# The sums of the second product's weight quarters, made by GpSimd beside the mixers instead of by VectorE before the product

## What is computed

```python
h = rms_norm(x, norm_w[layer]); proj = jnp.einsum('bsd,de->bse', h, w_in[layer])
(gq, gk, gv, glr, hq, hf, hi, xq, gate) = jnp.split(proj, split_idx, axis=-1)
# 4 heads of gated linear attention, with a gate from glr by a low-rank product,
# 4 recurrent heads (hgrn), 4 heads of cross attention on a memory of 256 tokens
mixed = jnp.concatenate([gla_o, hgrn_o, xo], axis=-1) * jax.nn.silu(gate)
x = x + jnp.einsum('bse,ed->bsd', mixed, w_out[layer])
```

```python
def sq_relu_mlp(h, w1, w2):
    return jnp.square(jax.nn.relu(h @ w1)) @ w2      # w1 1024 x 4096, w2 4096 x 1024
```

## Time and the profile before

| | us |
|---|---|
| median of 3 runs | 1999.69 |
| lowest and highest run | 1998.44, 2000.65 |
| the profiled execution, its own time | 1998.49 |
| its span, first to last instruction | 1996.7 |
| TensorE busy | 1964.0 (98%) |
| VectorE, ScalarE, GpSimd busy | 1254.3, 852.9, 927.4 |

### The profile page before, as it was taken

The page is one execution under the profiler, slowest core; times in us unless marked ns, Lnnn a source line. Parts: engine busy times, 40 slices in busy tenths (PEclk is TensorE's granted clock), DMA queues, the critical chain, the costliest instruction groups (busy, mean ns, idle before and its releaser), DMA issues.

```text
span 1996.7 us, 26700 instructions
## 1 busy us (share of the span) xinstructions
PE 1964.0 (98%) x10042; PEld 1649.4 (83%) x10042; DVE 1254.3 (63%) x2095; ACT 852.9 (43%) x1431; POOL 927.4 (46%) x584
## 2 busy tenths in 40 slices
PE   9999999999999999999999999999999999999997
PEld 7988988988988888888888777777788888888886
DVE  6264455446546365555579988896561845778856
ACT  5524232343543632121455557575643534333321
POOL 4521211112121334344428886686443855877851
PEclk9999999999999999999999999999999999999999
DMA  4301101011011596766335443334457886453432
GB/s 182 106 31 53 43 33 53 33 54 38 27 64 39 178 331 228 255 238 240 127 134 193 180 139 111 119 128 142 143 169 282 307 295 206 137 185 135 142 114 85
DMA packets 94047, 284.34 MB, mean 142 GB/s; under 512 B 10576, under 2 KB 10960, under 8 KB 93792
## 3 DMA queue, kind: packets, MB, share of 16 engines
q1 hardware_dynamic: 70736, 240.17, 35.0%
q10 hardware_dynamic: 23184, 42.48, 5.9%
HBM read 223.36 MB, written 59.24 MB: 142 GB/s over the span
## 4 chain that ended last, share of the span: by engine, by line
PE 59%; DVE 3%; ACT 3%; issue 2%; POOL 1%; DMA 0%; POOLq 0%; DVEq 0%; SPq 0%; ACTq 0%
PE B L1775 33%; PE B L2005 13%; PE B L1954 10%; PE B L2080 1%; DVE HB L2546 1%; POOL WL L3118 1%; PE B L2016 0%; ACT HB L2205 0%; DVE B L2546 0%; POOL CO L3177 0%; DMA SUMW<-wall 0%; DVE RES L2546 0%; DVE TM L2546 0%; ACT CO L2490 0%; PE B L1939 0%
## 5 line engine op out<-in xcount | busy, mean ns | idle before, releaser
L1775 PE MATMUL B<-HB,WH 128*128 128x512 f32 x2976 | 949.5, 401 | 6.3 <-ACT HB L2205 3.6
L1775 PEld LDWEIGHTS B<-HB,WH 128*128 128x128 f32 x2976 | 548.0, 189 | 129.2 <-issue 18.7
L1775 PE MATMUL B<-HB,WL 128*128 128x512 f32 x1488 | 578.0, 391 | 1.8 <-POOL WL L3118 1.8
L3118 POOL TENSOR_TENSOR WL<-RAW,WH 128x1024 fp32r<-128x1024 f32 x132 | 320.2, 2430 | 351.0 <-ACT WH L2205 349.3
L2205 ACT ACTIVATE WH<-RAW 128x1024 fp32r<-128x1024 f32 (+1 forms) x201 | 204.7, 1024 | 316.1 <-DMA RAW<-wall 298.4
L1775 PEld LDWEIGHTS B<-HB,WL 128*128 128x128 f32 x1488 | 279.6, 188 | 62.8 <-POOL WL L3118 3.1
L3116 POOL TENSOR_TENSOR WL<-RAW,WH 128x512 fp32r<-128x512 f32 x82 | 113.8, 1412 | 315.7 <-ACT WH L2205 315.6
L2546 DVE SCALAR_TENSOR_TENSOR B<-UP,vec,B 128x512 f32<-128x512 f32 x308 | 206.3, 747 | 0.0
L2546 DVE SCALAR_TENSOR_TENSOR RES<-B,modv,RES 128x512 f32<-128x512 f32 x204 | 148.0, 743 | 81.8 <-PE B L2005 59.1
L1838 PE MATMUL B<-WH,HB 128*128 128x256 f32 x768 | 153.2, 297 | 0.0
L3103 POOL TENSOR_TENSOR small<-small 128x4 f32<-128x4 f32 (+2 forms) x36 | 38.4, 1069 | 210.3 <-DVE small L2549 210.0
(11 more groups left out here) (270 smaller groups left out, 3330.5 us busy)
## 6 DMA issues: line engine op xcount, KB each, us to landing
RAW<-wall SPq DMA_DIRECT2D x172, 512.0 KB, 3.7
MODRAW<-wmod ACTq DMA_DIRECT2D x96, 256.0 KB, 4.9
WH<-parts SPq DMA_DIRECT2D x32, 512.0 KB, 3.2
WL<-parts SPq DMA_DIRECT2D x32, 512.0 KB, 4.1
hscr<-HR ACTq DMA_DIRECT2D x64, 256.0 KB, 3.2
HQ<-hscr SPq DMA_DIRECT2D x32, 512.0 KB, 6.4
SUMW<-wall SPq DMA_DIRECT2D x28, 512.0 KB, 7.3
sums<-SUMR SPq DMA_DIRECT2D x25, 512.0 KB, 5.9
```

Of the source, the lines that this page charges most:

```text
L1775: i = pe.matmul(bank, a[:, ks], hb(part, k, h), start=k == 0 and n == 0, stop=k == 7 and n == 2)
L3118: i = po.tensor_tensor(lo, raw, hi.bitcast(F32), ALU.subtract)
```

## The change

The sums move. The whole chain of load, four sums and store for each of the 28 units now runs beside the mixers, one unit at a time, in the tile GLR, from the place behind `gate_up` of head 3. Load, sums and store are placed 1.8, 1.6 and 1.6 planner us after one another. GpSimd makes the sums in place: S1 over A22, S3 over A21, S2 over A11, S4 over A12, so each unit keeps its four sums in the places of its quarters. All 28 are stored. Units 0 to 2 are loaded back too, ahead of the product. The later users of GLR's bytes and of the two semaphores (MXH1, the modulation's loads) wait for the last store or count past it.

```diff
-SUMS = ("S1", "S2", "S4", "S3")
+SUMS = ("S1", "S3", "S2", "S4")
+SUM_STEP = (1.8, 1.6, 1.6)
+LIES_IN = {"S1": "A22", "S2": "A11", "S3": "A21", "S4": "A12"}
...
+    sums_left = list(range(4 * LAST))
+    def sums_next():
+        if not sums_left:
+            return
+        n = sums_left.pop()
+        piece("s_load", n)
+        def add():
+            for t in SUMS:
+                piece("w_sum", n, t)
+            later(SUM_STEP[1], store)
+        def store():
+            piece("s_store", n)
+            later(SUM_STEP[2], sums_next)
+        later(SUM_STEP[0], add)
...
+        if h == 3:
+            sums_next()                      # behind gate_up of head 3
...
+    while P.kinds["s_store"] < 4 * LAST:     # behind the last cross head
+        next_due()
...
-            if h and f < 7:
-                sums_step()
-                next(sums, None)
+            if h and f < 5:
+                piece("sum_load", f - 2)     # second_product, second half
...
-            if h:
-                sums_step()                  # first_hidden and hidden, second half
...
-        if i == 4 * HG - 1:
-            for n in range(3):
-                sum_split(n)
+        if i >= 4 * HG - 3:
+            sum_split(i - 4 * HG + 3)
...
+            def w_sum(n, s):                 # now in GpSimd's program, gone from VectorE's
+                w.wait_ge(sig["d_side3"], 16 * (4 * LAST - n))
+                if s != "S1":
+                    w.wait_ge(sig["s_sum"], sums_made(n + 1) + SUMS.index(s))
+                a, b, op = {"S1": ("A21", "A22", ALU.add), "S3": ("A11", "A21", ALU.subtract),
+                            "S2": ("A22", "A11", ALU.subtract), "S4": ("A12", "A11", ALU.subtract)}[s]
+                po.tensor_tensor(sums_view(GLR, s), quarter(GLR, a), quarter(GLR, b), op).then_inc(sig["s_sum"], 1)
...
             def s_load(n):
-                if n + 3 < 4 * LAST:
-                    w.wait_ge(sig["s_sum"], sums_made(n + 3))
-                else:
-                    w.wait_ge(sig["z_lo"], 16)
+                if n + 1 < 4 * LAST:
+                    w.wait_ge(sig["d_side4"], 16 * (4 * LAST - 1 - n))
+                else:
+                    wait_full(w, "gate_up", 3, 0)
+                    wait_full(w, "gate_up", 3, 1)
             def s_store(n):
                 w.wait_ge(sig["s_sum"], sums_made(n))
-                sp.dma_start(sums[n, :, :], SUMR[n % 3][:, :]).then_inc(sig[f"d_side{n % 3}"], 16)
+                sp.dma_start(sums[n, :, :], GLR[:, :]).then_inc(sig["d_side4"], 16)
```

More of the change, by code:

```diff
@@ L48 @@
                 "pw2": 0.75, "sq_add": 0.65, "sq_add3": 0.7, "m1_mul": 0.66, "m1_lo": 0.66, "m2_mul": 0.75, "m2_lo": 0.85,
-                "w2_out": 0.75, "part_out": 0.75, "op_sum": 0.7, "w_sum": 0.35},
+                "w2_out": 0.75, "part_out": 0.75, "op_sum": 0.7},
         "pool": {"ptap": 1.45, "split": 2.5, "operand": 1.25}}
@@ L1124, in first_hidden @@
             hidden(i, h)
-            if h:
-                sums_step()
-    def sums_ahead():
-        for n in range(4 * LAST - 1, -1, -1):
-            if n + 3 < 4 * LAST:
[L1132 to L1137, removed]
     def sum_load(n):
@@ L1144, in sum_split @@
         piece("sum_split", n)
[L1146 to L1154, removed]
     rate[0] = 1.0
@@ L1202, in make_plan @@
     for i in range(GT, 4 * HG):
-        if i == 4 * HG - 2:
-            for _ in sums:
-                pass
-        if i == 4 * HG - 1:
-            for n in range(3):
-                sum_split(n)
+        if i >= 4 * HG - 3:
+            sum_split(i - 4 * HG + 3)
         hidden(i, 1)
@@ L1537, in build_program @@
         SUMR = [at(f"SUMR{i}", 1024, F32, x0 + (20 + 4 * i) * K2) for i in range(3)]
-        SUMW = [at(f"SUMW{i}", 1024, F32, x0 + (18 + 4 * i) * K2) for i in range(3)]
         HQ = [[at(f"HQ{r}{i}", 1024, F32, x0 + c * K2) for i, c in enumerate(cs)] for r, cs in enumerate(((30, 32), (34, 8)))]
@@ L1610, in sums_view @@
         def sums_view(t, s):
-            return t[:, 256 * int(s[1]) - 256:256 * int(s[1])]
+            return quarter(t, LIES_IN[s])
         def quarter(t, a):
@@ L1617, in quarter @@
             return t[:, o:o + 256]
+        SIDE_SUMS = 16 * 4 * LAST
         MOD_LOADS = [16 * len(range(i, 96, NMOD)) for i in range(3)]
-        def sum_turn(n):
-            return (4 * LAST - 1 - n) // 3
         def sums_made(n):
             return 4 * (4 * LAST - n)
-        def lane_total(i):
-            n = len(range(i, 4 * LAST, 3))
-            return MOD_LOADS[i] + 16 * (2 * n - 1)
         def wait_sum_there(w, n):
-            if n < 3:
-                w.wait_ge(sig["s_sum"], sums_made(n))
-            else:
-                w.wait_ge(sig[f"d_side{n % 3}"], lane_total(n % 3) + 16 * (n // 3))
+            w.wait_ge(sig[f"d_side{n % 3}"], MOD_LOADS[n % 3] + 16 * (n // 3 + 1))
         def wait_part(w, g, j2, m):
@@ L1992, in part @@
                     if a[0] == "S":
-                        c = 256 * int(a[1]) - 256 + 128 * r
+                        c = QUARTERS[LIES_IN[a]] + 128 * r
                     else:
@@ L2386, in mix_hi @@
                     wait_full(w, "x_score", 10, 7)
+                    w.wait_ge(sig["d_side4"], 16 * 4 * LAST)
                 copy(cut(MX[m][0], h), cut(ga, h)).then_inc(sig["mix_hi"], 1)
@@ L2771, in mod @@
                 acc, src = BANKS[5], MRAW[:, i % NMOD * 512:i % NMOD * 512 + 512]
-                w.wait_ge(sig[f"d_side{i % NMOD}"], 16 * (i // NMOD + 1))
+                w.wait_ge(sig[f"d_side{i % NMOD}"], 16 * (i // NMOD + 1) + SIDE_SUMS * (i % NMOD > 2))
                 if i:
@@ L3034, in split @@
                 tt(WL[:, c], RAW[:, c], WH[:, c].bitcast(F32), ALU.subtract).then_inc(sig[f"w_lo{q % NW}"], 1)
[L3036 to L3050, removed]
             def part_out(g, j2, m):
@@ L3088, in dve_program @@
                         m1_lo=m1_lo, m2_mul=m2_mul, m2_lo=m2_lo, glu=glu, tap=tap_, taps_end=taps_end,
-                        r1_dg=r1_dg, pre=pre, ysub=ysub, yadd=yadd, ln_r=ln_r, z_mul=z_mul, z_lo=z_lo, gbv=gbv, a2=a2, pw2=pw2, n3_sum=n3_sum, n3_row=n3_row, op_sum=op_sum, split=split, w_sum=w_sum, part_out=part_out,
+                        r1_dg=r1_dg, pre=pre, ysub=ysub, yadd=yadd, ln_r=ln_r, z_mul=z_mul, z_lo=z_lo, gbv=gbv, a2=a2, pw2=pw2, n3_sum=n3_sum, n3_row=n3_row, op_sum=op_sum, split=split, part_out=part_out,
                         w2_out=w2_out, n4_sum=n4_sum, n4_row=n4_row, final=final)
@@ L3193, in pool_program @@
             work = dict(split=split, x_sum=x_sum, m_sum=m_sum, rms=rms, mix_hi=mix_hi,
-                        n1_sum=n1_sum, pads=pads, ptap=ptap, ln_r=ln_r, n3_sum=n3_sum, n4_sum=n4_sum, operand=operand, sum_split=sum_split)
+                        n1_sum=n1_sum, pads=pads, ptap=ptap, ln_r=ln_r, n3_sum=n3_sum, n4_sum=n4_sum, operand=operand, sum_split=sum_split, w_sum=w_sum)
             po.memset(ones[:, :], 1.0).then_inc(sig["ones"], 1)
@@ L3223, in s_load @@
             def s_load(n):
-                if n + 3 < 4 * LAST:
-                    w.wait_ge(sig["s_sum"], sums_made(n + 3))
-                else:
-                    w.wait_ge(sig["z_lo"], 16)
-                sp.dma_start(SUMW[n % 3][:, :], wall[WALL.index(("w2", n // 4, n % 4)), :, :]).then_inc(sig[f"d_side{n % 3}"], 16)
+                if n + 1 < 4 * LAST:
+                    w.wait_ge(sig["d_side4"], 16 * (4 * LAST - 1 - n))
+                else:
+                    wait_full(w, "gate_up", 3, 0)
+                    wait_full(w, "gate_up", 3, 1)
+                sp.dma_start(GLR[:, :], wall[WALL.index(("w2", n // 4, n % 4)), :, :]).then_inc(sig["d_side3"], 16)
             def s_store(n):
                 w.wait_ge(sig["s_sum"], sums_made(n))
-                sp.dma_start(sums[n, :, :], SUMR[n % 3][:, :]).then_inc(sig[f"d_side{n % 3}"], 16)
+                sp.dma_start(sums[n, :, :], GLR[:, :]).then_inc(sig["d_side4"], 16)
             def sum_load(n):
-                w.wait_ge(sig[f"d_side{n % 3}"], lane_total(n % 3))
-                for m in (3, 5, 6, 7):
+                w.wait_ge(sig["d_side4"], 16 * 4 * LAST)
+                if n < 3:
+                    w.wait_ge(sig["z_lo"], 16)
+                for m in (3, 5, 6, 7) if n > 2 else ():
                     wait_part(w, (n - 3) // 4, (n - 3) % 4, m)
```

## The result

The changed kernel takes 2011.03 us (median of 4 runs, 2009.56 to 2012.97), the one before in the same comparison 1999.11 us: a ratio of 1.0048, 95% interval 1.0032 to 1.0063. That ratio gives 9.6 us and the medians give 11.9, so slower by 10 to 12 us. In a later comparison the ratio was 1.0060 (1.0047 to 1.0074). The forecast was 2007.7, slower, in 2000 to 2023.

A forecast was written before the change was run, and what follows sets the result against it. TensorE was taken as the bound. Old place 0, late chain 6.4 and GpSimd against VectorE 1.6 gave +8.0 us on 1998.49, 2006.5; with the median of the runs 1.2 higher, 2007.7, range 2000.0 to 2023.0.

The forecast's parts named there:

- Nothing to win in the old place: Between 1380 and 1700 us: removing sums, loads and stores gains at most 0.4 us of TensorE waits; booked 0.
- The turn of 10.2 us: Beside the mixers: load 3.4, four sums 3.3, store 3.2, hand-overs 0.3 us, 28 times over; bounds 9.1 to 12.1.
- Rival 2: Beside the mixers: chain sets the pace, by a 4 to 5 us store or more collisions; 2027 us; chance 0.22.
- rival 1: Beside the mixers: chain fits with turns of 9.7 us or less, leaving port contention of 1 to 3; about 2001.5; chance 0.20.
- The checkpoints: Three places in the mixers (turns 4, 9, 19) where the chain runs late; not added, 6.4 us stands for all.
- `rms` of head 8: Third checkpoint, turn 19: sums done at 470.5 for an `rms` that began at 460.59, 9.9 us late; 6.4 left.
- The first checkpoint: Turn 4, unit 23's sums ahead of `rms` of head 2: sums done at 311.5, TensorE loses about 2.5 us.
- weight loads late by up to 10 us cost TensorE nothing by themselves: In the mixers: a unit is loaded three units ahead of its use, so late loads cost 0.
- The second: Turn 9: load of weight unit 30 at 360.2 instead of 355.9, ScalarE's WH without slack, 6 us late in all.
- The price of the late chain: In the mixers: queues of SyncE and GpSimd wait in the chain, so the program is 6.4 us behind.
- The port: In the mixers: GpSimd's adds slow VectorE's instructions with two SBUF inputs; 1.6 us, lower bound 0.
- the bound of 14: Upper bound in us for port contention in the mixers, if half of the bursts each cost 1.0 us.

The follow-up runs named there:

- memset run: Changed kernel with each of the 112 GpSimd adds replaced by a GpSimd memset of 800 columns, chain kept; ratio 1.0032 to the kernel before.
- adds only: Changed kernel with 27 loads and all 28 stores left out beside the mixers, the 112 GpSimd adds kept; ratio 1.0048 to the kernel before.
- memsets only: Changed kernel without the 27 loads and all stores, each GpSimd add replaced by an 800-column memset; ratio 1.0005 to the kernel before.
- wide steps clear of `rms`: Changed kernel with steps 2.5, 2.3, 2.3 planner us and sums held back when an `rms` is due within 2.0; ratio 1.0069 to the kernel before.

## Why the prediction was right, and which terms were off

**Nothing to win in the old place: nearly.** I booked 0; without the sums anywhere the kernel is 2.4 us faster (0.4 to 4.4). What that gain consists of stays open: half may be the clock, and of TensorE's waits there 0.2 of 0.4 us went.

**The turn of 10.2 us: right.** Measured 9.4 to 10.2 where undisturbed; 11.4 on the mean of the 27, the longest 17.7. The store was shorter, 2.6 to 2.7 us to the next load instead of my 3.2 and 0.1. Rival 2's slow store is out, and rival 1 with it: the chain did not fit.

**The checkpoints: one of three held, by luck in its parts, and one was missed.** `rms` of head 8 was forecast at 470.5 and began at 470.94. But my order was off by one unit: unit 9's sums stand ahead of it, turn 18, not 19, and the first turn took 17.7 us (load to load, 262.92 to 280.66), since the first sums stood behind weight splits in GpSimd's queue until 274.42. The two errors cancel. The first checkpoint was wrong: unit 23's sums stand behind `rms` of head 2, which began at 307.78, 1.8 us late and not 5.5. TensorE is busy without a gap from 300 to 320 us, where I had it lose 2.5. The 1.8 were lost before, by the wait of 1.72 us at 294.67 for ScalarE, which stood behind a late weight unit; and that is a path I had put at nothing ("weight loads late by up to 10 us cost TensorE nothing by themselves"). The second was misread: the WH row at 359.23 is not that of the unit loaded at 355.91. In the changed kernel that load goes out at 358.63, near my 360.2, and this WH begins at 360.46, under 2 us later, so it was unit 29's. That slack I had denied is there, and TensorE's wait for OSB stayed 1.5 us. I also missed `rms` of head 5, which began at 529.28 for 514.77 before, directly behind the sums of unit 4; it cost TensorE nothing. The last store stands at 323.15 of the planner's clock, not at 315.8: each turn takes 5.76.

**The price of the late chain: 6.4 us forecast, 6.4 measured** with memsets (4.0 to 8.8). The size was right with wrong parts, so this was luck. I had three checkpoints hiding in one another. In the changed kernel's trace the chain costs TensorE 2.69 + 0.48 us of waits and 1.7 of clock at head 8 and 1.7 at 294 us: 6.6 in all. The memset run loses its time elsewhere, 2.76 us and a clock dip at 331, and shows no dip at head 8.

**The port: the term that was mis-sized.** 1.6 us forecast, 5.6 measured on top of the chain (with an uncertainty of 3 to 4) and 7 to 9 without it or with room, inside the bound of 14. These are prices against memsets, which hold up `scale` too. I scaled the small waits for VectorE in the earlier trace rows by GpSimd's time. That was the step that failed. The likely reason, which no run tests by itself, is that the old splits stand where they harm little while the adds go everywhere, and slack that is used up once doesn't scale. In the changed kernel's trace TensorE waits 1.04 us at 465, 0.68 at 483 and 1.08 at 512, each for VectorE instructions drawn out under a split or the adds. The rule of the Trainium skill (SBUF — State Buffer, section "SBUF: two separate sides"), an exclusive lock held for the whole instruction, which a VectorE instruction with two SBUF inputs meets only against a GpSimd instruction that reads SBUF, fits the runs: VectorE's product took 655 ns on the mean with the adds only and 481 with memsets only, and GpSimd, as busy with memsets that read nothing, cost 1.0 us.

**What the sum lacked: the clock.** Waits of 2.7 to 3.0 us came with up to 10 us of half the clock. At 475 us that cost 1.7 us. It isn't certain to come: behind the wait of 2.2 us in the memset run, at the same place, the clock stayed at 1.00. Single executions of the kernel before show dips as well (0.97), so of the 6.1 us that TensorE was busy longer only the 1.7 us at 475 can be put down to a wait of the chain, and over several executions the two kernels' clocks differ by under 2 us.

## What to carry to other kernels

A stretch whose engines all look half idle can still have no room: ask what each moved instruction stands directly ahead of in its queue, and who waits for that, before counting busy time. Price an added GpSimd instruction that reads SBUF tiles by what it does to VectorE's two-input instructions at that point, and test it with a memset of the same length; look in the trace whether the memset holds up something of its own. A total that agrees with the forecast says little about the parts: compare where the time was lost. Where order is written by a planner, one piece's place can be worth most of the effect (here 9 us of 12), so try neighbours before judging a move.

## What the runs showed of the hardware that was not expected

- After TensorE idled 3.2 of 5 us its granted clock over the next 5 us was 0.66. In the run with wide steps clear of `rms` it was 1.00 up to 615 us, when TensorE had stood for 0.9 us of a 2.99 us wait, and 0.50 from there to 625 (windows above).
- A 128x800 memset on GpSimd takes 0.77 us, about as long as an add of two 128x256 tiles (0.74), and leaves VectorE's two-input instructions at their bare time: the 128x256 product with TB took 481 ns on the mean with memsets only, 655 with adds only, 480 before. But it holds up a one-input instruction: four of `scale` over 128x256 took 2.90 us under memsets and 1.14 alone.
- Under a GpSimd subtract of 2.52 us a VectorE product of 128x128 took 2.42 us, and 0.28 alone.
- A 512 KB store to DRAM by itself lands in 2.6 us (the changed kernel's median over 28, up to 6.0), faster than the 512 KB load into the same tile (3.7).
